# Modulation weights as plain fp32 matmuls over four 32-column groups of the array, with a stream and buffers of their own

## The chip, the cores and the metric

The kernel runs on one core of a Trainium2 chip. A core has five engines that run side by side and meet only at semaphores: TensorE (PE in the profile; its weight loads have a row of their own, PEld), VectorE (DVE), ScalarE (ACT), GpSimd (POOL) and SyncE (SP), which here does nothing but issue transfers. Transfers run on 16 DMA engines. The metric is the device time of one execution in microseconds (us).

## What is computed

Two transformer blocks in float32, 1024 features. The first works on 256 latent tokens beside 256 context tokens (together 512, `NB`), the second on the 256 latent tokens alone (`S`). The part that the change touches is the modulation: nine vectors of 1024 features for each of two conditions, which scale, shift and gate the first block.

```
mod_lat = (silu(c) @ w_mod + b_mod)          # w_mod: 1024 x 9216
mod_ctx = (silu(c_ctx) @ w_mod + b_mod)
ml, mc = split(mod_lat, 9), split(mod_ctx, 9)
x  = x  + 0.5 * ml[2] * swiglu(rms_norm(x)  * (1 + ml[1]) + ml[0], ffn1_w_in, ffn1_w_out)
cx = cx + 0.5 * mc[2] * swiglu(rms_norm(cx) * (1 + mc[1]) + mc[0], ffn1_w_in, ffn1_w_out)
...                                          # ml[3], ml[4]: attention and conv; ml[5]: their gate
x  = x  + 0.5 * ml[8] * swiglu(rms_norm(x)  * (1 + ml[7]) + ml[6], ffn2_w_in, ffn2_w_out)
```

(The reference also multiplies each norm by its gain.) `w_mod` has 37.7 MB, the largest single matrix of the program. Only two columns of its product, one for each condition, are wanted.

## The kernel before

**Units.** All large weights come in units of 1 MB: 128 partitions by 2048 floats (`SLOT`), that is 8 chunks of 128 contracted rows (`kc`) by two tiles of 128 columns. `stream` holds the units in the order of use. SP loads a unit into one of the two halves of `raw` (`load`, L335). ACT copies each half of it to the matmul's rounded float format as `w_hi` (L466), and DVE subtracts to get the rest, `w_lo` (L839). A matmul is then made of three products, `x_hi*w_hi`, `x_lo*w_hi`, `x_hi*w_lo` (L1480 to L1482), which run in the one-pass format fp32r. `raw`, `w_hi` and `w_lo` are two units deep, so unit k+2 is split when unit k has been used.

**Modulation.** 36 of the units are `w_mod`, 256 columns each. For these the roles are turned around: the two conditions are the stationary operand, `sc_pad`, padded to 32 columns (hi parts in columns 0 and 1, lo parts in 2 and 3), and the weights are the moving one. So a modulation unit is 16 matmuls that move 256 columns (8 chunks, each with `w_hi` and `w_lo`, L1459 and L1460), all into partitions 0 to 31 of a bank of `ps_a`. DVE turns the result into features on partitions with 8 transposes of 32x32 (L865) and adds hi and lo (L868).

**The front.** The first 8 units (`MOD_FRONT`) are the shift and scale vectors of the first norm. They pass ACT, DVE and PE one after another, through `raw` and `wide_scr` in turn, while the tokens `x` land. Between them run the norm's statistics: ACT squares the tokens (L491), POOL sums six of the eight chunks (L392), PE sums over partitions (`stat`, L1443), ACT takes the root (L501), DVE builds a diagonal (L893, L896) and PE spreads it (`spread`, L1449). Then DVE forms the modulated tokens: z (L907), ACT adds the shift and rounds (`x_hi`, L514), DVE subtracts (`x_lo`, L918). The last three go chunk by chunk.

**ffn1.** 34 units of the first feed-forward layer, in slabs of 8, 8 and 6 hidden chunks, each followed by 4 output units. The other 28 modulation units (`MOD_RIDE`, 10 in a slab) ride between them: one behind each hidden unit and two behind the first outputs. Every hidden and output unit has 48 matmuls that move 512 columns (36 in the outputs of the last slab). Everything after ffn1 is untouched by the change.

**Order.** There is no scheduler: each engine's program is written out by hand, and each queue runs in that order. SP's loads wait for `l_ready` (DVE has split the unit that was in the buffer), splits wait for `halves_done` (PE has used `w_hi` and `w_lo`), PE waits for `l_ready` and `drained`.

Of the kernel before, what the change touches and what calls it, by code (L numbers as in the profile page):

```python
# [81 lines left out]
STAGES = (("front", MOD_FRONT), ("ffn1", 62), ("k", 1), ("v", 1), ("q", 4), ("gates", 8), ("conv", 8), ("bg", 4), ("merge", 8),  # L82
# [13 lines left out]
def program(nc, a, out):  # L96
    with ExitStack() as ctx:
# [25 lines left out]
        sc = sb("sc", [P, KD, 2])  # L123
        sc_pad = sb("sc_pad", [P, KD, MOD_ROWS], F32R)
# [88 lines left out]
        front_landed = [sem("front_landed0"), sem("front_landed1")]  # L213
# [4 lines left out]
        drained = sem("unit_drained")  # L218
        mod_turned = sem("mod_turned")
# [3 lines left out]
        sc_ready = sem("silu_c_ready")  # L223
# [13 lines left out]
        mods_ready = sem("mods_ready")  # L237
        gate_ready = sem("gate_ready")
# [80 lines left out]
        def landed_in(k):  # L319

            return wide_scr if k < MOD_FRONT and k // 2 % 2 else raw

# [7 lines left out]
        def _(sp):  # L330
# [16 lines left out]

            for u in range(MOD_FRONT + 2):
                if u >= 4:
                    sp.wait_ge(l_ready, 2 * u - 2)  # L350
                dst, landed = ((raw, raw_landed), (wide_scr, front_landed))[u // 2 % 2]
                sp.dma_start(dst[:, u % 2, :], a["stream"][u]).then_inc(landed[u % 2], LANDED)


            last_out = FIRST["k"] - 6
            run(MOD_FRONT + 2, last_out)
            for o in range(6):
                load(0, last_out + o, KD if o in (1, 3) else SLABS[2])
# [89 lines left out]
        def _(act):  # L448
# [6 lines left out]
            def split(pr, k, half):  # L455

                src = landed_in(k)
                if half == 0:
                    if src is raw:

                        act.wait_ge(raw_landed[k % 2], LANDED * pr + LANDED * (k // 2 + 1 - min(k, MOD_FRONT) // 4))
                    else:
                        act.wait_ge(front_landed[k % 2], LANDED * (k // 4 + 1))
                act.wait_ge(halves_done, 4 * pr + (2 * k + half + 1))
                cols = slice(half * HALF, (half + 1) * HALF)
                act.activation(w_hi[:, k % 2, cols], src[:, k % 2, cols], ACT.Copy).then_inc(h_ready, 1)  # L466
# [12 lines left out]
            act.wait_ge(vec_landed, 16)  # L479
            for i in range(2):  # L480
                act.activation(sc[:, :, i], vec[:, V_C + i * KD:V_C + (i + 1) * KD], ACT.Silu).then_inc(sc_ready, 1)
            act.wait_ge(sc_ready, 2)
            act.wait_ge(pad_ready, 1)
            act.activation(sc_pad[:, :, 0:2], sc[:], ACT.Copy).then_inc(pad_ready, 1)
            for u in range(2):
                splits(0, u)
# [5 lines left out]

            token_squares(0)
# [46 lines left out]
            for u in range(MOD_FRONT):  # L540
                splits(0, u + 2)
                if u == 0:
                    token_squares(1)
                    act.wait_ge(ident_landed, 16)
                    prepare_root()
                if u == 4:
                    roots(0, 4)
            act.dma_start(cst[:, K_R1:K_END], a["consts"][:, K_R1:K_END]).then_inc(cst_landed, 16)
            act.dma_start(late_w[:], a["late"]).then_inc(late, 16)
            norm_hi(0, NB, 0)  # L550
            act.wait_ge(cst_landed, 16)
            act.wait_ge(late, 16)
            act.activation(wg_hi[:], wg, ACT.Copy).then_inc(wg_done, 1)


            def slab1(s, pr, k, chunks, last):
                with act.Fori(0, chunks // 2) as p:
                    for j in range(2):
                        ki, m = k + 2 * j, 2 * p + j
                        split(pr + 2 * p, ki + 2, 0)  # L560
                        done(pr + 2 * p, ki)
                        act.activation(s1[:, j, :], bank(j, 0, NB), ACT.Silu).then_inc(silu_done, 1)
                        act.wait_ge(prod_done, 8 * s + m + 1)
                        act.activation(h_hi[:, m, :], t1[:, j, :], ACT.Copy).then_inc(hh_done, 1)
                        split(pr + 2 * p, ki + 2, 1)
                        splits(pr + 2 * p, ki + 3)
                for i, o in enumerate((0, None, 1, None, 2, 3)):
                    ko = k + 2 * chunks + i
                    if last and i == 1:
                        prepare_root()  # L570
                    if last and o is None:
                        squares(pr, ko - 1, i - 1, NB)
                    if last and o == 3:
                        squares(pr, ko - 1, 2 * o - 2, NB)
                        squares(pr, ko, 2 * o, NB)
                    else:
                        splits(pr, ko + 2)

            k = FIRST["ffn1"]
            with act.Fori(0, 2) as s:  # L580
                slab1(s, s * 11, k, SLABS[0], False)
            slab1(2, 0, k + 44, SLABS[2], True)
            roots(1, 4)
            norm_hi(1, NB, 3, FIRST["k"] + 1)
# [17 lines left out]


# [219 lines left out]
        def _(dve):  # L823
# [3 lines left out]
            dve.memset(sc_pad[:].bitcast(F32), 0.0).then_inc(pad_ready, 1)  # L827
# [5 lines left out]
            def split(pr, k, half):  # L833

                if half == 0:
                    dve.wait_ge(drained, 2 * pr + k)
                cols = slice(half * HALF, (half + 1) * HALF)
                dve.wait_ge(h_ready, 4 * pr + (2 * k + half + 1))
                dve.tensor_tensor(w_lo[:, k % 2, cols], landed_in(k)[:, k % 2, cols], w_hi[:, k % 2, cols].bitcast(F32),  # L839
                                  ALU.subtract).then_inc(l_ready, 1)  # L840
# [12 lines left out]
            dve.wait_ge(pad_ready, 2)  # L853
            dve.tensor_tensor(sc_pad[:, :, 2:4], sc[:], sc_pad[:, :, 0:2].bitcast(F32), ALU.subtract).then_inc(pad_ready, 1)
            dve.tensor_scalar(bm_half[:], bm, 0.5, None, ALU.mult).then_inc(vec_ready, 1)
            dve.tensor_tensor(gg[:], vec[:, V_F1:V_F1 + KD], vec[:, V_MIX:V_MIX + KD], ALU.mult).then_inc(vec_ready, 1)

            def mod(pr, k, m, b):

                done(pr, k)  # L860
                for q in range(P // MOD_ROWS):
                    rows = slice(q * MOD_ROWS, (q + 1) * MOD_ROWS)
                    for t in range(2):
                        lo = t * P + q * MOD_ROWS
                        ins = dve.transpose(turned[rows, b, t, :], ps_a[0:MOD_ROWS, b, lo:lo + MOD_ROWS])  # L865
# [1136 lines left out]
```

## Time and profile before

| what | value |
|---|---|
| time, median of 3 runs | 1393.19 us (1391.03 to 1394.19) |
| span of the profiled execution, first to last instruction | 1386.5 us |
| PE busy | 1319.4 us, 95% of the span |
| DVE busy | 854.4 us, 62% |
| ACT busy | 660.6 us, 48% |
| POOL busy | 61.9 us, 4% |
| DMA moved | 213.97 MB, mean 154 GB/s |
| modulation matmuls (L1459 and L1460) | 576 |

The page gives no device time for the profiled execution, only its span; the span is 6.7 us (0.5%) below the median, and the part outside it lies before the first and behind the last instruction. PE's busy time counts overlapping matmuls once, and matmuls are pipelined, so what a matmul costs in a stream is the distance from its start to the next one's start, not its own duration. Times in the trace are microseconds from the start of the span.

### The profile page before, as it was taken

The numbers are of one execution on the slowest core, as the hardware profiler recorded it, in microseconds if no ns is written. First come the engines' busy times: TensorE is split into PE (matmuls) and PEld (weight loads), VectorE is DVE, ScalarE is ACT, GpSimd is POOL, SyncE is SP. The second block draws the span as 40 slices with busy tenths as digits, with TensorE's granted clock in tenths as the row PEclk, the third lists the DMA queues.
The fourth block names the chain that finished last, engine by engine and source line by source line (L and its number), as shares of the span: only waits on it lengthen the run. The fifth ranks groups of instructions, "written<-read, shape, count | busy, mean of one in ns | idle before, by whom it ended". The sixth has DMA issues, their size and how long they took to land.

```text
span 1386.5 us, 24438 instructions
## 1 busy us (share of the span) xinstructions
PE 1319.4 (95%) x8912; PEld 1196.8 (86%) x8912; DVE 854.4 (62%) x1610; ACT 660.6 (48%) x958; POOL 61.9 (4%) x72
## 2 busy tenths in 40 slices
PE   5799999999999899999999899999899998899997
PEld 4588888888888689988999799999788888899997
DVE  6956644665457565677665555555657766666664
ACT  5544424442335334644434555645335565444542
POOL 2000000000000100000001000002002300000001
PEclk8899999999999899999999999999899999999998
DMA  8354444544344233432444455555432225355542
GB/s 334 133 182 155 163 139 149 170 156 159 121 182 152 91 122 137 166 122 94 149 171 163 182 182 182 184 182 171 161 108 107 99 84 182 122 182 190 182 173 91
DMA packets 30947, 213.97 MB, mean 154 GB/s; under 512 B 3376, under 2 KB 4656, under 8 KB 5936
## 3 DMA queue, kind: packets, MB, share of 16 engines
q1 hardware_dynamic: 30032, 209.73, 42.9%
q10 hardware_dynamic: 864, 3.56, 0.7%
q8 instruction: 32, 0.52, 0.2%
q14 instruction: 19, 0.16, 0.0%
HBM read 212.23 MB, written 1.05 MB: 154 GB/s over the span
## 4 chain that ended last, share of the span: by engine, by line
PE 86%; DVE 6%; ACT 3%; DMA 3%; issue 2%; POOL 0%; ACTq 0%; DVEq 0%; SPq 0%; POOLq 0%
PE ps_u L1480 25%; PE ps_u L1482 24%; PE ps_u L1481 24%; PE ps_a L1459 2%; PE ps_a L1460 2%; DVE w_lo L839 2%; DMA raw<-in_stream 2%; ACT w_hi L466 1%; PE ps_a L1432 1%; DMA x<-in_tokens 1%; PE ps_a L1699 1%; PE ps_a L1443 1%; PE ps_a L1636 1%; PE ps_a L1621 1%; PE ps_a L1795 1%
## 5 line engine op out<-in xcount | busy, mean ns | idle before, releaser
L839 DVE TENSOR_TENSOR w_lo<-raw,w_hi 128x1024 fp32r<-128x1024 f32 x386 | 470.7, 1228 | 269.5 <-ACT w_hi L466 266.0
L1480 PE MATMUL ps_u<-x_hi,w_hi 128*128 128x256 f32 (+1 forms) x1744 | 545.4, 313 | 23.2 <-DVE x_lo L918 12.9
L466 ACT ACTIVATE w_hi<-raw 128x1024 fp32r<-128x1024 f32 x386 | 399.3, 1052 | 303.1 <-PE ps_u L1482 164.0
L1481 PE MATMUL ps_u<-x_lo,w_hi 128*128 128x256 f32 (+1 forms) x1744 | 539.3, 309 | 0.0
L1482 PE MATMUL ps_u<-x_hi,w_lo 128*128 128x256 f32 (+1 forms) x1744 | 539.2, 309 | 0.0
L1480 PEld LDWEIGHTS ps_u<-x_hi,w_hi 128*128 128x128 f32 x1744 | 337.7, 194 | 46.1 <-issue 27.2
L1481 PEld LDWEIGHTS ps_u<-x_lo,w_hi 128*128 128x128 f32 x1744 | 337.9, 194 | 15.2 <-issue 0.5
L1482 PEld LDWEIGHTS ps_u<-x_hi,w_lo 128*128 128x128 f32 x1744 | 337.4, 193 | 15.7
L1480 PE MATMUL ps_u<-h_hi,w_hi 128*128 128x256 f32 (+1 forms) x800 | 245.5, 307 | 0.6 <-DVE h_lo L1043 0.6
L1481 PE MATMUL ps_u<-h_lo,w_hi 128*128 128x256 f32 (+1 forms) x800 | 245.0, 306 | 0.0
L1482 PE MATMUL ps_u<-h_hi,w_lo 128*128 128x256 f32 (+1 forms) x800 | 245.0, 306 | 0.0
L1480 PEld LDWEIGHTS ps_u<-h_hi,w_hi 128*128 128x128 f32 x800 | 152.8, 191 | 7.8 <-DVE h_lo L1043 0.8
L1482 PEld LDWEIGHTS ps_u<-h_hi,w_lo 128*128 128x128 f32 x800 | 152.8, 191 | 6.9
L1481 PEld LDWEIGHTS ps_u<-h_lo,w_hi 128*128 128x128 f32 x800 | 152.8, 191 | 6.5
L1459 PE MATMUL ps_a<-w_hi,sc_pad 128*32 128x256 f32 x288 | 74.6, 294 | 18.2 <-DVE w_lo L839 9.6
L392 POOL TENSOR_TENSOR sq<-sq 128x512 f32<-128x512 f32 (+1 forms) x30 | 36.1, 1204 | 1023.4 <-ACT sq L524 1006.7
L1460 PE MATMUL ps_a<-w_lo,sc_pad 128*32 128x256 f32 x288 | 74.6, 294 | 0.0
L1459 PEld LDWEIGHTS ps_a<-w_hi,sc_pad 128*32 128x32 f32 x288 | 33.0, 114 | 24.7 <-DVE scr L868 10.2
L947 DVE SCALAR_TENSOR_TENSOR x<-ps_u,gate_half,x 128x256 f32<-128x256 f32 x72 | 30.3, 477 | 25.8 <-PE ps_u L1482 25.7
L466 ACT ACT_TABLE_LOAD x19 | 24.4, 1283 | 43.0 <-DMA raw<-in_stream 42.9
L865 DVE STREAM_TRANSPOSE scr<-ps_a 32x32 f32<-32x32 f32 x288 | 43.6, 184 | 1.4
L1460 PEld LDWEIGHTS ps_a<-w_lo,sc_pad 128*32 128x32 f32 x288 | 33.0, 115 | 6.6
(236 smaller groups left out, 879.7 us busy)
## 6 DMA issues: line engine op xcount, KB each, us to landing
raw<-in_stream SPq DMA_DIRECT2D x185, 1024.0 KB, 4.8
raw<-in_stream SPq DMA_DIRECT2D x8, 768.0 KB, 4.2
wide_scr<-in_stream SPq DMA_DIRECT2D x4, 1024.0 KB, 8.4
x<-in_tokens ACTq DMA_DIRECT2D x2, 1024.0 KB, 14.4
wide_scr<-in_cmp_w SPq DMA_DIRECT2D x2, 1024.0 KB, 9.1
sq<-in_cmp_w SPq DMA_DIRECT2D x2, 1024.0 KB, 7.9
out<-x SPq DMA_DIRECT2D x4, 256.0 KB, 2.3
cst<-in_consts ACTq DMA_DIRECT2D x1, 766.0 KB, 4.3
```

The costliest lines, as they stand in the source:

```text
L392: pool.tensor_tensor(sq[:, 0, 0:width], sq[:, 0, 0:width], sq[:, kc, 0:width], ALU.add).then_inc(sq_sums, 1)
L466: act.activation(w_hi[:, k % 2, cols], src[:, k % 2, cols], ACT.Copy).then_inc(h_ready, 1)
L839: dve.tensor_tensor(w_lo[:, k % 2, cols], landed_in(k)[:, k % 2, cols], w_hi[:, k % 2, cols].bitcast(F32), ALU.subtract).then_inc(l_ready, 1)
L865: ins = dve.transpose(turned[rows, b, t, :], ps_a[0:MOD_ROWS, b, lo:lo + MOD_ROWS])
L947: ins = dve.scalar_tensor_tensor(x[:, m + t, cols], bank(b, t, n)[:, cols], gate(m + t, s), x[:, m + t, cols], ALU.mult, ALU.add)
L1432: return pe.transpose(dst, src, ident[0:n, 0:n])
L1443: ins = pe.matmul(ps_a[:, 3, t:t + 1], sq[:, kc, t * P:(t + 1) * P], ones[:, 0:1], start=(kc == SUMMED and t == 0), stop=(kc == 0 and t == ...
L1459: pe.matmul(dst, sc_pad[:, kc, :], w_hi[:, k % 2, cols], start=(kc == 0), stop=False)
L1460: ins = pe.matmul(dst, sc_pad[:, kc, :], w_lo[:, k % 2, cols], start=False, stop=(kc == KD - 1))
L1480: pe.matmul(dst, wh, xh, start=(kc == 0), stop=False)
L1481: pe.matmul(dst, wh, xl, start=False, stop=False)
L1482: ins = pe.matmul(dst, wl, xh, start=False, stop=(kc == span - 1))
```

## The change

The modulation weights leave the stream of units. A second input, `mods`, holds 36 pieces of 1 MB, four (`MOD_QUARTERS`) to each of the nine vectors: a quarter is 256 contracted rows by all 1024 columns of one vector. They are loaded as they are into four slots, the two halves of `wide_scr` and two parts of `scr` (ridden ones into the first two alone), and nothing splits them: ACT's copy and DVE's subtraction go for them. PE multiplies them in plain fp32. The stationary operand is again `sc_pad` with 32 columns, now plain fp32 with the two conditions alone; a quarter is 8 matmuls moving 256 columns, 2 chunks by 4 groups, and group g writes partitions 32g to 32g+31 of the same bank. So the four groups lie on four different 32-column groups of the array, and a whole vector ends as 128 partitions by 256 columns, which DVE turns with one transpose (`modulation`).

```diff
-            def mod(pr, k, b, lag):
-
-                pe.wait_ge(drained, 2 * pr + (k + 3 - lag))
-                dst = ps_a[0:MOD_ROWS, b, 0:2 * P]
-                for kc in range(KD):
-                    if kc in (0, 4):
-                        pe.wait_ge(l_ready, 4 * pr + (2 * k + 5 + kc // 4))
-                    cols = slice(kc * 2 * P, (kc + 1) * 2 * P)
-                    pe.matmul(dst, sc_pad[:, kc, :], w_hi[:, k % 2, cols], start=(kc == 0), stop=False)
-                    ins = pe.matmul(dst, sc_pad[:, kc, :], w_lo[:, k % 2, cols], start=False, stop=(kc == KD - 1))
...
+            def mod(u, b, quarter, slot, landed, free):
+
+                pe.wait_ge(mod_landed[slot], landed)
+                if quarter == 0 and free:
+                    pe.wait_ge(mod_turned, free)
+                for kc in range(2):
+                    for g in range(P // MOD_ROWS):
+                        rows = slice(g * MOD_ROWS, (g + 1) * MOD_ROWS)
+                        lo = (kc * (P // MOD_ROWS) + g) * MOD_COLS
+                        ins = pe.matmul(ps_a[rows, b, 0:MOD_COLS], sc_pad[:, 2 * quarter + kc, :], mod_slots[slot][:, lo:lo + MOD_COLS],
+                                        start=(quarter == 0 and kc == 0), stop=(quarter == MOD_QUARTERS - 1 and kc == 1))
+                ins.then_inc(mod_done, 1)
```

ffn1 becomes an instance of `swiglu`, the function that ffn2 had already. Its 34 units follow each other, and one quarter rides behind each of the first 28; PE's loop there is written out. Unit k+2 is now split while unit k+1 runs, with no modulation unit between.

```diff
+                if n == NB:
+                    for k, chunks in ((0, SLABS[0]), (12, SLABS[1]), (24, SLABS[2])):
+                        for o in range(chunks + 4):
+                            if o < chunks:
+                                unit(0, base + k + o, from_x(n), n, ready=normed(i))
+                            else:
+                                unit(0, base + k + o, from_h(n), n, chunks, ready=drained_at(0, base + k) if o == chunks else None)
+                            if k + o < MOD_RIDE:
+                                riding(k + o)
```

SP loads four quarters at once, then a unit, then the other four of the front as their slots come free; in ffn1 a unit and a quarter in turn. A quarter's load waits until PE has used the one two before it, and the loads queued behind it wait too.

```diff
+            for u in range(4):
+                mod_load(u, u)
+            load(0, 0, KD)
+            for u in range(4, MOD_FRONT):
+                sp.wait_ge(mod_done, u - 3)
+                mod_load(u, u - 4)
+            load(0, 1, KD)
+            with sp.Fori(0, MOD_RIDE // 2) as p:
+                for j in range(2):
+                    load(p, 2 + j, KD)
+                    sp.wait_ge(mod_done, 2 * p + (MOD_FRONT + j - 1))
+                    mod_load(2 * p + (MOD_FRONT + j), j)
```

In the front the scale vector comes first (`MOD_ORDER`), and `norm_lo` forms all eight z before it takes the shift vector (`between`).

```diff
+            dve.wait_ge(vec_ready, 1)
+            spread(0, 4)
+            modulation(0, 1, 0)
+            scale_of(0, 1, V_N1)
+            dve.wait_ge(scale_ready, 1)
+            splits(0, 0)
+
+            def after_scales():
+                modulation(1, 0, 1)
+
+            norm_lo(0, 0, NB, modulated(0, 1), 0, between=after_scales)
+            splits(0, 1)
```

**Where instructions move: DVE in the front.** Before, from the sixth modulation unit on; `scr` is the turned result, `t` the diagonal:

```order
L865 STREAM_TRANSPOSE scr<-ps_a 32x32 [waits halves_done]
L865 STREAM_TRANSPOSE scr<-ps_a 32x32 x7
L868 TENSOR_TENSOR scr<-scr 128x4 [waits mod_turned]
L839 TENSOR_TENSOR w_lo<-wide_scr,w_hi 128x1024 [waits w_hi_ready]
L893 RECIPROCAL rstd<-root 128x4 [waits root_done]
L896 TENSOR_SCALAR t<-cst,rstd 128x128 [waits recip_done]
L896 TENSOR_SCALAR t<-cst,rstd 128x128 x3
L839 TENSOR_TENSOR w_lo<-wide_scr,w_hi 128x1024 [waits w_hi_ready,unit_drained]
```

After, the same place, from the root to the first `x_lo`:

```order
L845 RECIPROCAL rstd<-root 128x4 [waits root_done,vec_ready]
L848 TENSOR_SCALAR t<-cst,rstd 128x128 [waits recip_done]
L848 TENSOR_SCALAR t<-cst,rstd 128x128 x3
L824 STREAM_TRANSPOSE turned<-ps_a 128x256 [waits mod_unit_done]
L827 TENSOR_TENSOR mods<-turned,vec 128x16 [waits mod_turned]
L833 SCALAR_TENSOR_TENSOR am<-mods,vec 128x16 [waits mods_ready]
L803 TENSOR_TENSOR w_lo<-raw,w_hi 128x1024 [waits w_hi_ready,unit_drained,scale_ready]
L803 TENSOR_TENSOR w_lo<-raw,w_hi 128x1024 [waits w_hi_ready]
L859 SCALAR_TENSOR_TENSOR sq<-x,am,ps_a 128x256 [waits rstd_spread]
L859 SCALAR_TENSOR_TENSOR sq<-x,am,ps_a 128x256 x15
L824 STREAM_TRANSPOSE turned<-ps_a 128x256 [waits mod_unit_done]
L827 TENSOR_TENSOR mods<-turned,vec 128x16 [waits mod_turned]
```

The splits of 8 modulation units are gone from DVE's queue, the root's diagonal stands first in it, and all 16 halves of z (`sq<-x,am,ps_a`) stand between the diagonal and the shift vector.

**PE in the front.** Before, behind the fourth modulation unit (`ones,sq` are the statistics):

```order
L1443 MATMUL ps_a<-ones,sq 128x1 [waits squares_summed]
L1443 MATMUL ps_a<-ones,sq 128x1 x3
L1459 MATMUL ps_a<-w_hi,sc_pad 32x256 [waits w_lo_ready,unit_drained]
L1460 MATMUL ps_a<-w_lo,sc_pad 32x256
L1459 MATMUL ps_a<-w_hi,sc_pad 32x256
```

After, behind the fourth quarter (`t,ones` is the spread):

```order
L1379 MATMUL ps_a<-ones,sq 128x1 [waits squares_summed]
L1379 MATMUL ps_a<-ones,sq 128x1 x3
L1396 MATMUL ps_a<-wide_scr,sc_pad 32x256 [waits mod_landed0]
L1396 MATMUL ps_a<-wide_scr,sc_pad 32x256 x7
L1396 MATMUL ps_a<-wide_scr,sc_pad 32x256 [waits mod_landed1]
L1396 MATMUL ps_a<-wide_scr,sc_pad 32x256 x7
L1385 MATMUL ps_a<-t,ones 128x512 [waits diag_done]
L1396 MATMUL ps_a<-scr,sc_pad 32x256 [waits mod_landed2]
```

What moved: the quarters wait for their transfers alone; the statistics stand behind the fourth quarter as they did behind the fourth unit, and the spread (L1385) behind the sixth instead of the seventh.

## Rows read from the trace of the kernel before

**Rows 1.** The page: busy time and instructions, and the chain's shares by engine.

```profile
PE 1319.4 (95%) x8912; PEld 1196.8 (86%) x8912; DVE 854.4 (62%) x1610; ACT 660.6 (48%) x958; POOL 61.9 (4%) x72
PE 86%; DVE 6%; ACT 3%; DMA 3%; issue 2%; POOL 0%; ACTq 0%; DVEq 0%; SPq 0%; POOLq 0%
```

**Rows 2.** Busy by stretch: PE, PEld, DVE, ACT, POOL, granted clock, DMA share, GB/s.

```profile
0.00:20.00 20.00, 5.55 (x32) 4.44 (x32) 9.29 (x23) 10.98 (x17) 4.78 (x7) 0.99 0.93 372
20.00:22.00 2.00, 1.75 (x8) 1.20 (x8) 1.97 (x2) 1.98 (x3) 1.76 (x2) 0.50 1.02 426
20.00:40.00 20.00, 17.62 (x105) 14.30 (x106) 18.34 (x52) 13.67 (x17) 3.36 (x2) 0.67 0.75 268
100.00:200.00 100.00, 100.00 (x497) 83.53 (x496) 56.81 (x118) 42.06 (x45) 0.00 (x0) 1.00 0.48 168
```

**Rows 3.** Timeline of PE in ffn1: start, duration, operation.

```profile
65.22 0.28 PE L1459 MATMUL ps_a<-w_hi,sc_pad 128*32 128x256 f32 x1
...
67.09 0.40 PE L1480 MATMUL ps_u<-x_hi,w_hi 128*128 128x512 f32 x1
...
77.97 0.28 PE L1459 MATMUL ps_a<-w_hi,sc_pad 128*32 128x256 f32 x1
```

**Rows 4.** PE around plain fp32 matmuls with 30 stationary columns.

```profile
1006.71 0.28 PE L1482 MATMUL ps_u<-x_hi,w_lo 128*128 128x256 f32 x1
1006.91 7.09 PE L1699 MATMUL ps_a<-sq,s 128*30 128x256 f32 x32
1013.94 0.38 PE L1480 MATMUL ps_u<-x_hi,w_hi 128*128 128x256 f32 x1
1014.16 0.28 PE L1481 MATMUL ps_u<-x_lo,w_hi 128*128 128x256 f32 x1
```

**Rows 5.** Weight loads at three entries: before L1459, L1699 and L1636.

```profile
65.00 0.11 PEld L1459 LDWEIGHTS ps_a<-w_hi,sc_pad 128*32 128x32 f32 x1
...
1006.91 0.35 PEld L1699 LDWEIGHTS ps_a<-sq,s 128*30 128x30 f32 x3
...
642.57 0.74 PEld L1636 LDWEIGHTS ps_a<-scr,sq 128*128 128x128 f32 x4
```

**Rows 6.** PE, plain fp32: full width, and two groups of 64 columns (L1736).

```profile
642.69 1.89 PE L1636 MATMUL ps_a<-scr,sq 128*128 128x256 f32 x8
644.41 1.88 PE L1621 MATMUL ps_a<-sq,q_cur 128*128 128x512 f32 x4
...
1027.48 0.42 PE L1736 MATMUL ps_a<-hid,late_w 128*64 128x15 f32 x8
```

**Rows 7.** DVE's timeline in the front; in brackets idle time and its releaser.

```profile
34.75 1.23 DVE L839 TENSOR_TENSOR w_lo<-wide_scr,w_hi 128x1024 fp32r<-128x1024 f32 x1 [0.19 <-ACT w_hi L466]
35.89 1.25 DVE L865 STREAM_TRANSPOSE scr<-ps_a 32x32 f32<-32x32 f32 x8
...
38.60 0.88 DVE L896 TENSOR_SCALAR t<-cst,rstd 128x128 f32<-128x128 f32 x4
...
48.72 1.66 DVE L907 SCALAR_TENSOR_TENSOR sq<-x,am,ps_a 128x256 f32<-128x256 f32 x4
50.56 0.88 DVE L918 SCALAR_TENSOR_TENSOR x_lo<-sq,mods,x_hi 128x256 fp32r<-128x256 f32 x2 [0.19 <-ACT x_hi L514]
```

**Rows 8.** The statistics: ACT, POOL and PE, same columns.

```profile
18.80 2.19 ACT L491 ACTIVATE sq<-x 128x512 f32<-128x512 f32 x4 [0.89 <-DMA x<-in_tokens]
...
21.51 2.09 POOL L392 TENSOR_TENSOR sq<-sq 128x512 f32<-128x512 f32 x1
...
29.62 2.88 PE L1443 MATMUL ps_a<-ones,sq 128*128 128x1 f32 x24
...
473.52 2.07 PE L1449 MATMUL ps_a<-t,ones 128*128 128x512 f32 x2 [1.48 <-DVE t L896]
```

**Rows 9.** The chain at ffn1's first matmul: start, duration, what.

```profile
51.59 0.76 PE ps_u L1480
```

**Rows 10.** DMA issues on the page: size, median us from issue to landing.

```profile
raw<-in_stream SPq DMA_DIRECT2D x185, 1024.0 KB, 4.8
```

More of the change, by code:

```diff
@@ L345, in run, with mod_load @@
                 units(first, end - first)
[L348 to L358, printed above, removed]
+            def mod_load(u, slot):
+                sp.dma_start(mod_slots[slot], a["mods"][u]).then_inc(mod_landed[slot], LANDED)
+            for u in range(4):
[10 more added lines that the diff above has]
+                    mod_load(2 * p + (MOD_FRONT + j), j)
+            units(2 + MOD_RIDE, 4, SLABS[2])
             run(FIRST["k"], FIRST["ffn2"])
@@ L479, in _ @@
             act.wait_ge(vec_landed, 16)
+            act.wait_ge(pad_ready, 1)
             for i in range(2):
[L481 to L486, printed above, removed]
+                act.activation(sc_pad[:, :, i], vec[:, V_C + i * KD:V_C + (i + 1) * KD], ACT.Silu).then_inc(pad_ready, 1)
             def token_squares(half):
@@ L537, in out_step @@
                     splits(pr, k0 + i + 2)
[L540 to L547, printed above, removed]
+            token_squares(0)
+            token_squares(1)
+            act.wait_ge(ident_landed, 16)
+            prepare_root()
+            roots(0, 4)
+            splits(0, 0)
@@ L548, in _ @@
+            act.wait_ge(mods_ready, 2)
+            norm_hi(0, NB, 0)
             act.dma_start(cst[:, K_R1:K_END], a["consts"][:, K_R1:K_END]).then_inc(cst_landed, 16)
             act.dma_start(late_w[:], a["late"]).then_inc(late, 16)
[L550 to L577, printed above, removed]
@@ L897, in spread, with norm_lo @@
                 ins.then_inc(diag_done, 1)
-            def norm_lo(n, i, width, scale, shift, at=0, held=None):
+            def norm_lo(n, i, width, scale, shift, at=0, held=None, between=None):
                 dve.wait_ge(rb_done, n + 1)
@@ L920, in lo @@
                     ins.then_inc(xl_ready, 1)
-                z(0)
+                ahead = 1 if between is None else KD
+                for kc in range(ahead):
+                    z(kc)
+                if between is not None:
+                    between()
                 for kc in range(KD):
-                    if kc + 1 < KD:
-                        z(kc + 1)
+                    if kc + ahead < KD:
+                        z(kc + ahead)
                     if held is not None and kc == 5:
@@ L1023, in _ @@
[L1023 to L1029 removed]
+            dve.wait_ge(vec_ready, 1)
[3 more added lines that the diff above has]
+            dve.wait_ge(scale_ready, 1)
+            splits(0, 0)
@@ L1054, in _ @@
+            swiglu(FIRST["ffn1"], 0, NB, 0)
+            dve.wait_ge(wg_done, 1)
+            dve.tensor_tensor(wg_lo[:], wg, wg_hi[:].bitcast(F32), ALU.subtract).then_inc(wg_ready, 1)
+            spread(1, 4)
+            dve.wait_ge(scale_ready, 3)
+            dve.wait_ge(gate_ready, 2)
+            norm_lo(1, 1, NB, modulated(1, 4), 3, held=FIRST["k"] + 1)
             k = FIRST["k"]
```

254 lines of the change are left out of this document (91 added, 163 removed).

## Prediction

> **What bounds the kernel now.** I read the page first: PE is busy 95% of the span, and 86% of the chain that ended last is PE's [rows 1]. Then the table by stretch, which shows two regimes [rows 2]. From 100 us on PE is busy in every microsecond at full clock while DVE stands at 57%: ffn1 is bound by PE alone. In the first 50 us it is not: PE is busy 5.55 of the first 20 us, and DVE 18.34 of the next 20. There DVE is the bound, because each modulation unit costs it two subtractions of 1.23 us and 1.25 us of transposes [rows 7]. The first matmul of ffn1 starts at 51.59 [rows 9]. So there are two sums: what a ridden quarter costs PE in ffn1 against a ridden unit, 28 times, and how early ffn1 starts. Behind ffn1 nothing changes.
>
> **ffn1: what is removed.** A ridden unit takes PE from 65.22 to 67.09, 1.87 us for 16 matmuls (0.117 each, and nothing for turning from 128 columns to 32 and back) [rows 3]. 28 x 1.87 = 52.4 us, all on the path. The hidden unit between two of them takes 10.88 us (67.09 to 77.97) and stays.
>
> **ffn1: what is added.** A plain fp32 matmul appears in the trace as two records. L1636 has 4 in a row as 8 records from 642.69 until the next line starts at 644.41: 0.215 us a record at 256 columns, 0.43 a matmul [rows 6]. With 30 stationary columns it is the same: L1699's 32 records take 7.03 us with what surrounds them [rows 4]. A quarter is 8 matmuls, 16 records. No row shows fp32 matmuls of this size on different column groups, so their cost is bounded from both sides. Above: no overlap, 16 x 0.215 = 3.44 us. Below: a group has 2 matmuls of its own, 4 records, 0.86 us, which is what remains if all four groups run at once. Between them lies what I take. In every row of the timeline PE's matmuls start in program order. The program has both records of a group next to each other, and the second uses the same 32 columns as the first, so it starts 0.215 later; if the next group's first record may not start before it, only these two run together. Then 8 matmuls take 9 record times, 1.94 us. The nearest rows, L1736, are two groups of 64 columns with 15 moving ones: 8 records in 0.42, the last of them about 0.21 long, so one each 0.03 us with no jump at the change of group [rows 6]; they are too short to tell.
>
> To this comes entering and leaving. Before L1459 and L1636 the first weight load starts under the preceding matmul (65.00 against 65.22, 642.57 against 642.69); before L1699 it starts with its own matmul at 1006.91, 0.20 after the last fp32r matmul instead of 0.12 [rows 4, 5]. Behind it the first matmul comes at 1013.94, 7.03 after the first, where 32 x 0.215 = 6.88, and its successor 0.22 later instead of 0.12. So narrow plain fp32 is another mode of the array, entered and left through an empty pipe, for 0.08 + 0.15 + 0.10, less what L1699's own pitch explains: I take 0.24 a visit, 0.15 to 0.35 as its bounds. The Trainium skill says so too (TensorEngine Tiling (Array Packing), Key Properties): changing the tiling mode drains the array. The trace agrees, with 0.08 us at entry; the rule speaks against the change, since before there were no such visits.
>
> A ride then costs 1.94 + 0.24 = 2.18 us, 0.31 more than now: 28 x 0.31 = **+8.7 us**. The Trainium skill (TensorE: Matmul & The Clock Gate, Part 3: Packing small matmuls — row/col tiling) gives 2.38x for three column groups at once, type not told; an estimate from that page is 3.44 / 2.38 + 0.24 = 1.69 us a ride, -5 us in place of +8.7. No run here shows it.
>
> **The front.** Eight modulation units leave ACT and DVE, so the statistics and the transfers set the pace. The order of events: 8 quarters, 2 MB of tokens and a unit are 11.5 million bytes; the first 20 us move 372 GB/s [rows 2], which makes 31 us from issue to the last quarter. That isn't last. The second half of the tokens is squared from 18.80 [rows 8]; one more megabyte is queued beside it, so I take 19.5. POOL's last sum ended at 23.60 [rows 8], now 24.3. PE's last third of `stat` is a third of 2.88 us: 25.3. Root, reciprocal and diagonal, 0.88 for the last [rows 7] and an estimate of 0.6 for the others and the handoffs: 26.8. Meanwhile DVE turns the scale vector (an estimate of 0.7 us from the 1.25 for eight small transposes) and subtracts for unit 0: until 30.0. PE has run quarters 5 and 6, and since it stood idle before `stat` its clock may be at the lower of its two levels, 0.50 of full as at 20 to 22 us [rows 2]: until 31.5, then the spread, 0.9 to 2.07 [rows 8]: 33. Then 16 halves of z at 0.415 (1.66 for four [rows 7]) make 6.6: 39.6. All this hides quarters 7 and 8. Then the shift vector, 0.6, and `x_hi` and `x_lo` of one chunk. Before, those two took from 49.55 (48.72 plus half of 1.66) to 51.59, 2.0 [rows 7, 9]: **42.2** instead of 51.59, **-9.4 us**, bounds -7 and -12. The first unit then runs at half clock as now, since PE idles before it in both. `x_lo` now comes each 0.88 us instead of each 1.6, but PE needs 1.36 a chunk, so this buys nothing more.
>
> **What costs nothing.** In ffn1 ACT and DVE lose the splits of 28 units; they are busy 42% and 57% there beside a full PE [rows 2], so nothing is gained. DVE's wait for a vector's last quarter stands behind the fourth hidden unit; queued behind it is the split of a unit that PE wants a whole unit (10.9 us) later. SP's wait for the ride two before holds back a unit's load, but its own condition, the split of the unit in its buffer, comes later anyway. The riding quarter is issued some 10 us before its use, against 4.8 us to landing in the median [rows 10]; should that cover go, a ride waits up to 5 us. The 2 MB a unit pair are the bytes of before.
>
> **Sum.** -9.4 + 8.7 = -0.7 us. The profile's span is 1386.5; against the median of 1393.19 the difference holds as it is: **1392.5 us**. Its own range is 1383 to 1402.
>
> **Rivals.**
> A, *four groups at once*: 0.86 + 0.24 = 1.10 a ride, -0.77 x 28 = -21.6 us; the front gains 11, since quarters 5 and 6 are short: 1360.6 us. For it: the narrow mode exists, as the gap at L1699 shows, and two records that only need different columns have no visible reason to queue. Against it: program order of starts. The Trainium skill (TensorEngine Tiling (Array Packing), Key Properties) states that tiles execute in parallel; by that rule alone it is A. The Trainium skill (TensorE: Matmul & The Clock Gate, Part 3) adds that matmuls keep their order at start and end, which with the first gives my case; in the trace the starts do keep it.
> B, *no overlap at all*: 3.44 + 0.24 = 3.68 a ride, +1.81 x 28 = +50.7 us. In the front quarters 7 and 8 end at about 40.7 and set ffn1's start to 43.3, -8.3. 1435.6 us, slower. It decides from a quarter of 2.3 us on. For it: every fp32 row of the trace has this pace, and none shows two matmuls sharing the array. Against it: only the mode's name.
> C, *the rides stall* on their transfer or SP's order, at 1 us a ride: 1392.5 + 28 = 1420.5, or more. The front's order of loads speaks for it a little, the 10 us of cover against it.
>
> **How the numbers follow.** My case 0.40, A 0.28, B 0.28, C 0.04. What a measurement of this kernel can tell from no change is about 0.2%, 2.8 us. My own case straddles it: faster 0.17, same 0.11, slower 0.12. So faster is 0.28 + 0.17 = 0.45, same 0.11, slower 0.12 + 0.28 + 0.04 = 0.44. Leaving out A or B would leave out more than 2 in 10, so the range takes in both with their bounds: 1356 to 1440.
>
> **What would show it.** In the profile after, the distance from the first matmul of a quarter to the next unit's first is the whole question: 2.2 us is my case, 1.1 is A, 3.7 is B. The starts inside a quarter tell the mechanism: in mine two records start together each 0.215 us, in A four. The start of ffn1 should be near 42 us, with the 16 z just ahead of it and the shift vector behind them. ffn1 should show PE busy throughout; idle time before a quarter, released by its transfer, would be C. Wrong at the root would be a front held by something other than the tokens, or a gap behind ffn1 that isn't there now.

## The result, and the profile after

The changed kernel takes **1359.47 us** (median of four runs, 1358.1 to 1362.85) against 1392.59 (four runs, 1391.03 to 1394.19): a ratio of 0.9771, 95% interval 0.9757 to 0.9786, or 33.1 us less. That lies inside the range of the prediction, but 33 us below its likeliest case. It is the time of rival A (1360.6), and the trace shows A's mechanism: the four column groups work at once. That the two times agree to about 1 us is partly luck: A's terms were off by up to 4.8 us, and these errors and the scatter between executions cancel (see the sum below).

The page of after, with the chain's shares and the loads of the new stream:

```profile
span 1358.8 us, 23503 instructions
PE 1298.6 (96%) x8912; PEld 1153.2 (85%) x8912; DVE 728.0 (54%) x1217; ACT 589.9 (43%) x885; POOL 59.9 (4%) x72
PE 85%; DVE 6%; ACT 4%; DMA 2%; issue 2%; DVEq 0%; ACTq 0%; SPq 0%
wide_scr<-in_mods SPq DMA_DIRECT2D x32, 1024.0 KB, 6.7
```

The number of PE's instructions is the same as before [rows 1], DVE has 393 fewer and 126 us less to do, and PE is still what the chain runs through. By stretch (length, busy time with counts of PE, PEld, DVE, ACT, POOL, then granted clock, DMA share, GB/s):

```profile
0.00:20.00 20.00, 6.90 (x60) 2.46 (x64) 1.58 (x8) 4.68 (x9) 4.17 (x8) 1.00 0.91 368
20.00:40.00 20.00, 12.80 (x99) 8.06 (x92) 12.28 (x32) 7.29 (x14) 2.34 (x2) 0.89 0.91 376
100.00:200.00 100.00, 100.00 (x537) 76.45 (x536) 33.33 (x46) 27.78 (x31) 0.00 (x0) 1.00 0.44 168
```

DVE fell from 18.34 to 12.28 us in the second 20 us [rows 2]; in ffn1 PE is full as before, so that DVE went from 57% to 33% there gained the kernel nothing.

Now a ridden quarter in PE's timeline (start, duration, operation; a row with x16 is sixteen records together):

```profile
51.76 0.39 PE L1423 MATMUL ps_u<-x_hi,w_lo 128*128 128x512 f32 x1
52.08 1.07 PE L1396 MATMUL ps_a<-wide_scr,sc_pad 128*32 128x256 f32 x16
53.08 0.50 PE L1421 MATMUL ps_u<-x_hi,w_hi 128*128 128x512 f32 x1
53.42 0.40 PE L1422 MATMUL ps_u<-x_lo,w_hi 128*128 128x512 f32 x1
53.66 0.40 PE L1423 MATMUL ps_u<-x_hi,w_lo 128*128 128x512 f32 x1
...
64.23 1.07 PE L1396 MATMUL ps_a<-wide_scr,sc_pad 128*32 128x256 f32 x16
```

Sixteen records take 1.00 us to the next line's first, where one after another at 0.215 they would take 3.44. How they lie is seen in stretches of 0.01 us, matmuls and weight loads of L1396 alone:

```profile
52.12:52.13 0.01, 0.01 (x4) 0.01 (x8) 1.00 0.00 0
52.30:52.31 0.01, 0.01 (x4) 0.00 (x0) 1.00 0.00 0
52.35:52.36 0.01, 0.01 (x8) 0.01 (x4) 1.00 0.00 0
52.51:52.52 0.01, 0.01 (x4) 0.00 (x0) 1.00 1.93 819
52.55:52.56 0.01, 0.01 (x8) 0.01 (x4) 1.00 0.00 0
52.73:52.74 0.01, 0.01 (x4) 0.00 (x0) 1.00 0.00 0
52.77:52.78 0.01, 0.01 (x8) 0.00 (x0) 1.00 1.93 819
```

Four matmul records run at 52.12. Just after 52.30 four more have joined (the eight are the old four, whose modelled ends overlap, and the new), and again after 52.51 and after 52.73: waves of four, about 0.215 us apart. The counts don't name the groups, but one record of each group at a time, four waves in all, is what fits them, and the first three experiments below bear it out.

**Where the 27.7 us between the two spans are** (1386.5 to 1358.8). The first matmul of ffn1 starts at 39.68 instead of 51.59 [rows 9]: -11.9. From there to the last matmul of ffn1 it is 395.71 us instead of 414.02: -18.3. The way from ffn1 to the next unit (L1421) is 1.4 longer, the rest 1.1 longer. The rows of before and then of after, and below them a stretch of after with the granted clock behind POOL's numbers:

```profile
465.61 0.39 PE L1482 MATMUL ps_u<-h_hi,w_lo 128*128 128x512 f32 x1
468.41 3.64 PE L1443 MATMUL ps_a<-ones,sq 128*128 128x1 f32 x24 [2.41 <-ACT sq L524]
...
478.58 0.76 PE L1480 MATMUL ps_u<-x_hi,w_hi 128*128 128x512 f32 x1 [2.98 <-DVE x_lo L918]
```

```profile
435.39 0.39 PE L1423 MATMUL ps_u<-h_hi,w_lo 128*128 128x512 f32 x1
438.19 5.04 PE L1379 MATMUL ps_a<-ones,sq 128*128 128x1 f32 x24 [2.41 <-ACT sq L515]
...
449.80 0.77 PE L1421 MATMUL ps_u<-x_hi,w_hi 128*128 128x512 f32 x1 [3.01 <-DVE x_lo L870]
```

```profile
438.20:439.00 0.80, 0.80 (x5) 0.80 (x6) 0.46 (x2) 0.71 (x2) 0.00 (x0) 0.68 0.00 0
```

The 24 small matmuls behind ffn1 start after the same 2.80 us but take 5.04 instead of 3.64. In both traces the clock is still 1.00 when they start and falls to 0.50 while they run; by the means of the stretches (0.68 from 438.20 to 439.00 in after, 0.92 from 469.40 to 470.40 in before) it fell about 0.3 us after their start in after and about 1.8 us in before. That is no cost of the change, for it moves as much between kernels that are the same there. Read from the trace of each kernel in this document, in us (the first unit without the 0.09 us of entry to the ride behind it):

| trace | first matmul of ffn1 | first unit | end of ffn1 to the next unit | rest |
|---|---|---|---|---|
| before | 51.59 | 13.63 | 12.97 | 907.9 |
| after | 39.68 | 12.31 | 14.41 | 909.0 |
| all on one group | 40.18 | 12.88 | 12.99 | 907.7 |
| on two groups | 40.69 | 13.07 | 12.49 | 906.6 |
| order exchanged | 40.50 | 12.96 | 14.23 | 906.0 |
| a quarter of the work | 40.26 | 12.87 | 13.32 | 911.2 |
| 14 visits | 39.67 | | 14.56 | 905.6 |
| 7 visits | 40.41 | | 14.65 | 908.4 |
| four z ahead | 36.92 | 12.58 | 14.10 | 906.5 |
| 7 visits, four z ahead | 36.44 | | 12.43 | 906.6 |

The seven from after to 7 visits have the same front. So of the four terms of the 27.7 us, the front's is 10.9 to 11.9 and only the rides' comes out the same each time; what lies behind ffn1 scatters by 2.2 and by 5.6 us around before's values.

In every run on record whose time and span are both listed, 1.8 us of the time lie outside the span (1360.61 with span 1358.8 for the profiled one of after). So the profiled execution of before was one of about 1388.3, 4.3 below its median of 1392.59 and below all four times listed there, while that of after was 1.1 above its own. These two make up the difference between the traces' 27.7 and the medians' 33.1.

### The profile page after: what moved, and what is told of

The parts are those of the page before. It is cut to its first block, busy times and chain, and to the rows that moved or that the text cites. A ratio compares the mean times of both kernels' runs of the same rounds, so it can differ in the third digit from the quotient of the medians.

```text
span 1358.8 us, 23503 instructions
## 1 busy us (share of the span) xinstructions
PE 1298.6 (96%) x8912; PEld 1153.2 (85%) x8912; DVE 728.0 (54%) x1217; ACT 589.9 (43%) x885; POOL 59.9 (4%) x72
## 4 chain that ended last, share of the span: by engine, by line
PE 85%; DVE 6%; ACT 4%; DMA 2%; issue 2%; DVEq 0%; ACTq 0%; SPq 0%
PE ps_u L1421 25%; PE ps_u L1422 25%; PE ps_u L1423 24%; PE ps_a L1396 2%; ACT w_hi L463 1%; PE ps_a L1379 1%; DVE w_lo L803 1%; PE ps_a L1368 1%; DMA scr<-in_mods 1%; DMA raw<-in_stream 1%; PE ps_a L1626 1%; DVE sq L859 1%; PE ps_a L1563 1%; PE ps_a L1548 1%; PE ps_a L1722 1%
## 5 line engine op out<-in xcount | busy, mean ns | idle before, releaser
L1421 PE MATMUL ps_u<-x_hi,w_hi 128*128 128x256 f32 (+1 forms) x1744 | 548.1, 314 | 20.7 <-DVE x_lo L870 11.6
L803 DVE TENSOR_TENSOR w_lo<-raw,w_hi 128x1024 fp32r<-128x1024 f32 x322 | 394.1, 1228 | 300.5 <-ACT w_hi L463 296.6
L463 ACT ACTIVATE w_hi<-raw 128x1024 fp32r<-128x1024 f32 x322 | 337.6, 1054 | 318.1 <-PE ps_u L1423 280.1
L1421 PEld LDWEIGHTS ps_u<-x_hi,w_hi 128*128 128x128 f32 x1744 | 338.1, 194 | 52.6 <-issue 33.4
L1421 PE MATMUL ps_u<-h_hi,w_hi 128*128 128x256 f32 (+1 forms) x800 | 246.5, 308 | 0.5 <-DVE h_lo L944 0.5
L1421 PEld LDWEIGHTS ps_u<-h_hi,w_hi 128*128 128x128 f32 x800 | 152.8, 191 | 11.2 <-issue 3.7
L941 DVE TENSOR_TENSOR t<-s,ps_u 128x512 f32<-128x512 f32 (+1 forms) x44 | 24.4, 553 | 93.0 <-ACT s L549 93.0
L549 ACT ACTIVATE s<-ps_u 128x512 f32<-128x512 f32 (+1 forms) x44 | 21.5, 488 | 100.7 <-PE ps_u L1423 100.6
L903 DVE SCALAR_TENSOR_TENSOR x<-ps_u,gate_half,x 128x256 f32<-128x256 f32 x72 | 30.4, 477 | 33.1 <-PE ps_u L1423 33.0
L1396 PE MATMUL ps_a<-wide_scr,sc_pad 128*32 128x256 f32 x512 | 37.2, 413 | 7.0 <-ACT sc_pad L479 6.9
L944 DVE TENSOR_TENSOR h_lo<-t,h_hi 128x256 f32 (+2 forms) x44 | 24.6, 559 | 35.9 <-ACT h_hi L551 35.9
L551 ACT ACTIVATE h_hi<-t 128x512 f32 (+1 forms) x44 | 23.1, 525 | 36.7 <-DVE t L941 36.7
L1396 PEld LDWEIGHTS ps_a<-wide_scr,sc_pad 128*32 128x32 f32 x512 | 14.3, 115 | 24.8 <-issue 19.0
```

The lines of the kernel that those rows point to most:

```text
L463: act.activation(w_hi[:, k % 2, cols], raw[:, k % 2, cols], ACT.Copy).then_inc(h_ready, 1)
L549: act.activation(s1[:, j, 0:n], bank(k + j, 0, n), ACT.Silu).then_inc(silu_done, 1)
L551: act.activation(h_hi[:, 2 * p + j, 0:n], t1[:, j, 0:n], ACT.Copy).then_inc(hh_done, 1)
L803: dve.tensor_tensor(w_lo[:, k % 2, cols], raw[:, k % 2, cols], w_hi[:, k % 2, cols].bitcast(F32), ALU.subtract).then_inc(l_ready, 1)
L903: ins = dve.scalar_tensor_tensor(x[:, m + t, cols], bank(b, t, n)[:, cols], gate(m + t, s), x[:, m + t, cols], ALU.mult, ALU.add)
L941: dve.tensor_tensor(t1[:, j, 0:n], s1[:, j, 0:n], bank(k + j, 1, n), ALU.mult)\
```

## Experiments

Eight kernels. Beside the first four before took 1390.68, beside the last four 1391.69, and the ratios are to these. After was not run again beside them, so a difference to after is one of medians, and 1 or 2 us of it mean little. The questions: do the groups really run beside each other, by which rule, what does a visit to them cost beyond the stream, and what sets the front.

**All ridden matmuls on one group.** The ridden product is then not the reference's, since four parts add up in one place.

```diff
-                        rows = slice(g * MOD_ROWS, (g + 1) * MOD_ROWS)
+                        r = g if u < MOD_FRONT else g % 1
+                        rows = slice(r * MOD_ROWS, (r + 1) * MOD_ROWS)
...
-                                        start=(quarter == 0 and kc == 0), stop=(quarter == MOD_QUARTERS - 1 and kc == 1))
+                                        start=(quarter == 0 and kc == 0 and r == g), stop=(quarter == MOD_QUARTERS - 1 and kc == 1 and (u < MOD_FRONT or g >= 3)))
```

> The changed kernel, but all 8 matmuls of a ridden quarter write partitions 0 to 31, so they share one column group (the modulation values of ffn1 are then not the reference's). If the gain comes from four groups working at the same time, a ride goes from 1.27 us to 16 x 0.215 + 0.41 = 3.85 us and the kernel gets 28 x 2.58 = 72 us slower than the changed one, 1432 us. If narrow plain fp32 were simply faster than its rows before had shown, whatever the group, it stays at 1359 us.

It took 1429.69 us (one run). PE's timeline:

```profile
67.83 3.64 PE L1397 MATMUL ps_a<-wide_scr,sc_pad 128*32 128x256 f32 x16
...
82.50 3.64 PE L1397 MATMUL ps_a<-wide_scr,sc_pad 128*32 128x256 f32 x16
```

A period is 14.67 us. Less the 10.88 of a hidden unit [rows 3], a ride is 3.79, against 12.15 - 10.88 = 1.27 in after. The same sixteen records, loads and transfers cost 2.52 us more when they share 32 columns; 28 times that is 70.6, and the time rose by 70.2. So it is the distribution over column groups that makes the ride cheap.

**On two groups**, 0 and 1 in turn; part of the product is wrong for the same reason. The edit is the one above with these lines (and `g >= 2` in `stop`).

```diff
+                        r = g if u < MOD_FRONT else g % 2
...
```

> The changed kernel with the ridden matmuls on column groups 0, 1, 0, 1 (values again not the reference's). If a ride lasts as long as its busiest group, 8 records: 1.72 + 0.41 = 2.13 us, 28 x 0.86 = 24 us more than the changed kernel, 1383 us. If records started strictly in program order, as the prediction had it, 9 record times: 1.94 + 0.41 = 2.35 us, 1390 us.

1380.62 us (one run):

```profile
66.81 1.92 PE L1397 MATMUL ps_a<-wide_scr,sc_pad 128*32 128x256 f32 x16
...
79.76 1.92 PE L1397 MATMUL ps_a<-wide_scr,sc_pad 128*32 128x256 f32 x16
```

The period is 12.95, a ride 2.07. Eight records of the busier group are 1.72, and 0.35 is left, as in the run on one group (3.79 - 3.44). What counts is the load of the busiest group; what the prediction took, that only the two records at a change of group meet, would give 1390, 9.4 us more than the one run took.

**Order exchanged.** After writes groups 0, 1, 2, 3 with the quarter's first matmul and again with its second. Here each group's two matmuls stand together, so that the one behind must wait for its group.

```diff
-                for kc in range(2):
-                    for g in range(P // MOD_ROWS):
+                order = [(kc, g) for kc in range(2) for g in range(4)] if u < MOD_FRONT else [(kc, g) for g in range(4) for kc in range(2)]
+                for kc, g in order:
...
```

> The changed kernel with the two loops of a ridden quarter exchanged: both chunks of group 0, then both of group 1, and so on; same work, same groups. If every group has a queue of its own, nothing changes: 1.27 us a ride, 1359 us. If whole matmuls start in program order and one that finds its group taken holds up those behind it, the second of each group blocks the next group: 5 matmul times of 0.43, 2.15 + 0.41 = 2.56 us a ride, 28 x 1.29 = 36 us more, 1396 us. If single records did so (the prediction's step), 13 record times, 2.80 + 0.41 = 3.21 us, 1414 us.

1358.95 us (two runs), ratio to before 0.977 (0.9733 to 0.9808), the same as after:

```profile
65.72 1.09 PE L1397 MATMUL ps_a<-wide_scr,sc_pad 128*32 128x256 f32 x16
...
77.88 1.09 PE L1397 MATMUL ps_a<-wide_scr,sc_pad 128*32 128x256 f32 x16
```

1.28 us a ride. If a matmul that waits for its group held back those behind it, this order would have shown it, with 2.56 or more. It doesn't. Stretches of 0.01 us show the same waves as in after, four records at first and then eight, of which four are running out:

```profile
65.85:65.86 0.01, 0.01 (x4) 0.01 (x5) 1.00 0.00 0
65.99:66.00 0.01, 0.01 (x8) 0.01 (x4) 1.00 0.00 0
```

In program order the first four records are two matmuls of one group, and records of one group ran one after another in the run on one group. So a record for a free group starts although an earlier one in the program still waits for a busy one.

**A quarter of the work**: only group 0's two matmuls of a ridden quarter, 4 records instead of 16; three quarters of the ridden product are left out.

```diff
-                    for g in range(P // MOD_ROWS):
+                    for g in range(P // MOD_ROWS if u < MOD_FRONT else 1):
```

> The changed kernel with only group 0's two matmuls of each ridden quarter; the other three groups' products are left out, so three quarters of the ridden modulation values are wrong. If four groups run fully beside each other, the time of the ride's own records does not change (4 x 0.215 us) and the kernel stays at 1359 us. If the slower matmuls behind a ride (0.34 and 0.24 us apart instead of 0.227, 0.30 us in all) come from the number of instructions just issued, they shrink, and it is up to 28 x 0.2 = 5 us faster, 1354 us; if they come from leaving the narrow mode, they stay.

1362.52 us (two runs), ratio 0.9796 (0.9759 to 0.9833): not faster than after. That it is 3 us slower lies outside the rides: its trace has as long an ffn1 (395.70 us against 395.71) and 2.2 us more in the last column of the table above, which scatters.

```profile
65.34 1.05 PE L1396 MATMUL ps_a<-wide_scr,sc_pad 128*32 128x256 f32 x4
66.32 0.50 PE L1421 MATMUL ps_u<-x_hi,w_hi 128*128 128x512 f32 x1
66.66 0.40 PE L1422 MATMUL ps_u<-x_lo,w_hi 128*128 128x512 f32 x1
...
77.47 1.05 PE L1396 MATMUL ps_a<-wide_scr,sc_pad 128*32 128x256 f32 x4
```

A ride of 1.25 us for 4 records against 1.27 for 16: three of the four groups ride for nothing. The slow steps behind the visit (0.34 us to the next line, then 0.24 instead of 0.227) are there unchanged, so they come with leaving the visit, and not with the number of instructions in it. The 1354 of the other reading is refuted.

**Fewer visits.** Two quarters behind every second unit, in four buffers (14 visits), and four quarters behind every fourth (7 visits). The second is shown; the first has `% 2 == 1` and two `riding` calls in the last lines, and the same loads and buffers:

```diff
-            with sp.Fori(0, MOD_RIDE // 2) as p:
-                for j in range(2):
-                    load(p, 2 + j, KD)
-                    sp.wait_ge(mod_done, 2 * p + (MOD_FRONT + j - 1))
-                    mod_load(2 * p + (MOD_FRONT + j), j)
+            with sp.Fori(0, MOD_RIDE // 4) as p:
+                for j in range(4):
+                    load(2 * p, 2 + j, KD)
+                    sp.wait_ge(mod_done, 4 * p + (MOD_FRONT + j - 3))
+                    mod_load(4 * p + (MOD_FRONT + j), j)
...
-                mod(u, (c - 2) % 3, u % MOD_QUARTERS, n % 2, LANDED * (n // 2 + 3), c - 2)
+                mod(u, (c - 2) % 3, u % MOD_QUARTERS, n % 4, LANDED * (n // 4 + 3), c - 2)
...
-                            if k + o < MOD_RIDE:
-                                riding(k + o)
+                            if k + o < MOD_RIDE and (k + o) % 4 == 3:
+                                for r in range(4):
+                                    riding(k + o - 3 + r)
```

> The changed kernel with two quarters behind every second unit instead of one behind each, and four slots for the ridden quarters. Same matmuls, 14 visits to the narrow mode instead of 28. A ride costs 1.27 us and its own records 0.86, so a visit costs 0.41: 14 x 0.41 = 5.7 us less than the changed kernel, 1353.7 us. If the 0.41 belonged to the matmuls and not to the visit, it stays at 1359.5 us.

> Four quarters, a whole vector, behind every fourth unit: 7 visits. By the cost of a visit, 21 x 0.41 = 8.6 us less than the changed kernel, 1350.9 us. Against it: the four loads come in one row and a slot is free only after the visit, so a visit could wait for its last transfer; that would show as idle time of PE before it.

14 visits took 1352.83 us (four runs, 1351.5 to 1354.23; ratio 0.9721, 0.9697 to 0.9744), 7 visits 1351.48 (1347.61 to 1352.94; 0.9698, 0.9672 to 0.9725). A visit in the first, then one in the second:

```profile
63.37 1.93 PE L1396 MATMUL ps_a<-wide_scr,sc_pad 128*32 128x256 f32 x32
...
87.22 1.93 PE L1396 MATMUL ps_a<-scr,sc_pad 128*32 128x256 f32 x32
```

```profile
86.20 1.93 PE L1396 MATMUL ps_a<-wide_scr,sc_pad 128*32 128x256 f32 x32
...
89.79 0.50 PE L1421 MATMUL ps_u<-x_hi,w_hi 128*128 128x512 f32 x1
...
133.53 1.93 PE L1396 MATMUL ps_a<-wide_scr,sc_pad 128*32 128x256 f32 x32
```

Two quarters cost 23.85 - 2 x 10.88 = 2.09 us instead of 2 x 1.27, so a visit saved is 0.45 us. Four cost 47.33 - 4 x 10.88 = 3.81 (3.59 of it up to the next line) instead of 4 x 1.27, which is 0.42 for each of three visits saved. Fourteen visits fewer at 0.45 are 6.3 us, measured 6.6; twenty-one fewer at 0.42 are 8.8, measured 8.0. So the fixed cost belongs to the visit and not to the matmuls. From 14 visits to 7 the intervals overlap, and that step is not measured on its own by the times.

**The shift vector earlier in the front**: four z ahead of it instead of all of the unit.

```diff
-                ahead = 1 if between is None else KD
+                ahead = 1 if between is None else 4
```

> The changed kernel with the shift vector taken after four z instead of all eight, so DVE's queue holds 8 fewer halves of z ahead of it. The last front quarter is done at 33.5 us and DVE would turn it at about 33.9 instead of 36.96: ffn1 starts near 36.7 us instead of 39.68, 3 us less, 1356.5 us. If the front is held by something else (the transfer of the last quarter, or x_lo, which then comes every 1.6 us at first), the start stays within 1 us of 39.7 or the first unit gets longer by as much.

1357.11 us (four runs, 1355.33 to 1358.55; ratio 0.9751, 0.9729 to 0.9774). DVE's rows and PE's first matmul of ffn1:

```profile
31.12 3.22 DVE L859 SCALAR_TENSOR_TENSOR sq<-x,am,ps_a 128x256 f32<-128x256 f32 x8 [0.49 <-PE ps_a L1385]
34.26 0.44 DVE L824 STREAM_TRANSPOSE turned<-ps_a 128x256 f32<-128x256 f32 x1
...
36.92 0.72 PE L1421 MATMUL ps_u<-x_hi,w_hi 128*128 128x512 f32 x1 [3.08 <-DVE x_lo L870]
```

The first matmul comes 2.76 us earlier than in after, and earlier than in all seven traces with the old front (39.67 to 40.69); the first unit takes 0.27 longer. So z really stood on the path in after. The time falls by 2.4, but its interval overlaps that of after, so the time alone would not show it.

**Both together**, 7 visits and four z ahead:

> Both edits together, four quarters a visit and the shift vector after four z. They lie in different stages, so they should add: 8.6 + 3.0 = 11.6 us less than the changed kernel, 1348 us.

1346.53 us (1344.35 to 1349.44), ratio 0.9679 (0.9654 to 0.9704): 45 us under before and 13 under after, the fastest of the kernels here. ffn1 starts at 36.44.

The two gains (8.0 and 2.4) add up to 10.4, and 12.9 was measured: nothing shows that they take from each other. The second edit alone, on top of 7 visits, moved ffn1's start by 4.0 us and the time by 5.0, so by these two pairs its worth lies between 2.4 and 5.0.

## Why the prediction was right or wrong

The measured time lies in the range because the range was made to take in rivals A and B; the case that the prediction held likeliest did not happen.

**The step that failed** is the one from the starts' order to the overlap: "if the next group's first record may not start before it, only these two run together". It made nine record times of a ride. The rows on which it stood show matmuls that follow each other on the same columns, the whole array or one narrow group (L1459, L1699), or, in L1736, 0.42 us in which no wave could be told from another [rows 6]; that the starts follow the program there says nothing on matmuls for free columns. The waves in after, the ride's 3.79, 2.07 and 1.27 us on one, two and four groups, and the exchanged order show that a ride lasts as long as its busiest group: 4 records, 0.86 us predicted in rival A and 0.89 measured. B is refuted by the same rows.

**The visit** was mis-sized: 0.24 us taken, 0.15 to 0.35 as bounds, 0.41 measured in after, 0.35 in the rides on one and two groups, and 0.42 to 0.45 for each visit taken away. The ride of 1.27 is 0.09 at entry, 0.89 for four waves, 0.11 at exit, and 0.18 in the matmuls behind, whose distances begin with 0.34, 0.24, 0.24 where 0.227 is usual. The last term is what the prediction lacked: it read L1699's exit only to the first successor [rows 4]. The Trainium skill (TensorEngine Tiling (Array Packing), Key Properties) says that a change of the tiling mode drains the engine; the trace agrees with its 0.09 and 0.11 us, and the slow matmuls behind are not in that rule.

By these sizes ffn1 gives 28 x (1.27 - 1.87) = -16.8 instead of +8.7, and rival A's -21.6 was 4.8 too hopeful, all of it in the visit. The other -1.3 of ffn1 is its first unit, 12.31 us instead of 13.63: it was told to run at half clock as before, and it does at first, but the clock rose about 2.9 us after its first matmul instead of about 5.6 (in before it was 0.50 until 57 and 0.88 from 57 to 58). In the traces of the other kernels this unit takes 12.58 to 13.07, so 0.3 to 0.8 of the 1.3 belongs to this one execution; before has only one trace, and what sets the rise stays open. Three stretches of after show it: two of a microsecond, where the clock (the number behind POOL's) rises from 0.50 to 0.73, and then the whole first unit at a mean of 0.88, where before had 0.79:

```profile
41.00:42.00 1.00, 1.00 (x4) 0.71 (x4) 1.00 (x4) 1.00 (x3) 0.00 (x0) 0.50 0.76 313
42.00:43.00 1.00, 1.00 (x5) 0.82 (x4) 1.00 (x3) 1.00 (x4) 0.00 (x0) 0.73 0.94 356
39.68:52.08 12.40, 12.40 (x48) 9.90 (x49) 8.99 (x17) 9.98 (x17) 0.00 (x0) 0.88 0.58 200
```

**The front** was right in its mechanism and nearly in size: -11.9 against -9.4, at the end of its bounds of -7 to -12 (-10.9 to -11.9 over the seven traces with this front). Here ACT, PE and DVE of after, in order of time:

```profile
19.10 2.19 ACT L484 ACTIVATE sq<-x 128x512 f32<-128x512 f32 x4 [2.78 <-DMA x<-in_tokens]
```

```profile
20.83 5.28 PE L1379 MATMUL ps_a<-ones,sq 128*128 128x1 f32 x24
26.04 3.31 PE L1396 MATMUL ps_a<-wide_scr,sc_pad 128*32 128x256 f32 x32
29.28 1.13 PE L1385 MATMUL ps_a<-t,ones 128*128 128x512 f32 x2
32.41 1.07 PE L1396 MATMUL ps_a<-scr,sc_pad 128*32 128x256 f32 x16 [1.01 <-DMA scr<-in_mods]
39.68 0.76 PE L1421 MATMUL ps_u<-x_hi,w_hi 128*128 128x512 f32 x1 [6.19 <-DVE x_lo L870]
```

```profile
27.52 0.44 DVE L824 STREAM_TRANSPOSE turned<-ps_a 128x256 f32<-128x256 f32 x1
28.41 2.36 DVE L803 TENSOR_TENSOR w_lo<-raw,w_hi 128x1024 fp32r<-128x1024 f32 x2
30.69 6.35 DVE L859 SCALAR_TENSOR_TENSOR sq<-x,am,ps_a 128x256 f32<-128x256 f32 x16
36.96 0.44 DVE L824 STREAM_TRANSPOSE turned<-ps_a 128x256 f32<-128x256 f32 x1
```

The tokens came at 19.1 (taken: 19.5), the statistics ended at 26.1 (25.3), unit 0's split at about 30.7 (30.0); these hold within a microsecond. The term that was off is the spread: predicted at 33 because quarters 5 and 6 were to run until 31.5, but both together take 3.31 us, since their groups overlap too, and it is done at 30.4. Then the split, not the spread, is what z waits for in this trace, and z starts at 30.69. The two are close: in 14 visits it is the split too, but in the other five traces with this front z starts at 31.18 to 31.69, behind the spread, for which DVE stands idle 0.53 to 0.89 us. So the predicted path through the spread holds in most traces, about 2 us too late. The z themselves take 6.27, to 36.96 (6.6 predicted), and from there it is 2.72 to the first matmul (2.6). The last quarter lands only for a start at 32.41 (31 predicted), hidden behind z as said. In rival A, with short quarters, the same list gave 40.6. How much of the gain comes from the splits that are gone, how much from taking the scale vector first and how much from the order of z was not measured apart.

**What costs nothing** held: in ffn1 PE has no idle time before a quarter, so no ride stalls (rival C), and the new stream's loads take 6.7 us to landing against some 10 of cover. **Behind ffn1** the two traces differ by 2.5 us (1.4 up to the next unit and 1.1 over the 909 us that follow), but these stretches scatter as much between kernels that are the same there, so nothing on record speaks against the statement that nothing changes.

**The sum** was right in form. With the terms of these two traces it reads: front -11.9, rides -16.8, first unit -1.3, behind +2.5, and -0.2 of remainder, -27.7. Rival A had -11 and -21.6, -32.6 in all: nearly the medians' 33.1, with rides 4.8 too cheap. The last step, "against the median of 1393.19 the difference holds as it is", is weaker than it was put. Only 1.8 of the 6.7 us between the span of before and that median lie outside the span; the other 4.9 are scatter between executions, so two traces can't stand for two medians to better than a few us.

## What to carry to other kernels

Small-output matmuls in plain fp32 that are spread over the four 32-column groups cost what the busiest group costs, in both program orders that were tried: here three of four groups were free (1.27 us for 16 records against 1.25 for 4), and that beat the split into fp32r, which had the cheaper matmul. Count the visits as well as the work: each change from full-width matmuls to the groups and back cost 0.35 to 0.45 us, so gather what rides until buffers or due times forbid it. And where the rows of a trace show no case of a thing (two matmuls for different columns in a row), the order seen in other rows is no evidence on it. And before a microsecond is put down to a change, see whether the same stretch keeps its length between kernels that are the same there.

## What the runs showed of the hardware

- Plain fp32 at 32 columns on one, two and four groups: 3.79, 2.07 and 1.27 us for the same 16 records of 256 moving columns, that is 16, 8 and 4 times 0.215 and 0.35 to 0.41 of visit. The Trainium skill (TensorE: Matmul & The Clock Gate, Part 3: Packing small matmuls — row/col tiling) has 2.38x for three column groups; for four, these runs show 3.79 / 1.27 = 2.98x with the visit and 3.44 / 0.89 = 3.9x without. It also says that matmuls are never reordered in start or end; the ride in exchanged order (1.28 us, where waiting in order would make an estimated 2.56) doesn't agree with that for matmuls on different groups, and the measurement decides.
- Behind a visit the full-width matmuls are slow for some steps, 0.34 and then 0.24 us instead of 0.227, whether 4 or 16 records ran in it. What makes them slow stays open.
- Behind ffn1 the clock fell from 1.00 to 0.50 while the 24 matmuls of the statistics ran, about 0.3 us after their start in after and 1.8 in before; over ten traces the stretch from ffn1 to the next unit takes 12.43 to 14.65 us.
- One transpose of 128x256 on DVE takes 0.44 us, where eight of 32x32 took 1.25 [rows 7].
